# A 64x64 triangular inverse inside a decoder trunk: two products issued in four quarters of the array, the second with crossed heads

## What is computed

```python
def step(s, inp):
    r_t, w_t, k_t, v_t, z_t, bb_t = inp
    sz = jnp.einsum("bhij,bhj->bhi", s, z_t)
    s = s * w_t[:, :, None, :] + sz[..., None] * bb_t[:, :, None, :] + v_t[..., None] * k_t[:, :, None, :]
    return s, jnp.einsum("bhij,bhj->bhi", s, r_t)
```

## Time and profile before

| | |
|---|---|
| median of 3 runs | 1491.04 us |
| profiled execution, its own time | 1490.77 us |
| its span in the trace | 1489.0 us |
| TensorE (PE) busy | 1444.4 us, 97% |
| VectorE (DVE) busy | 830.7 us, 56% |
| ScalarE (ACT) busy | 509.8 us, 34% |
| chain that ended last, PE's share | 91% |

### The profile page before, as it was taken

How to read it: one execution, slowest core, us unless ns; L and a number is a source line. 1 busy time by engine, 2 the same in 40 slices (tenths; PEclk the granted TensorE clock), 3 DMA queues, 4 the chain that set the end, 5 groups by cost and what they waited for, 6 DMA issues and landing times.

```text
span 1489.0 us, 21859 instructions
## 1 busy us (share of the span) xinstructions
PE 1444.4 (97%) x9700; PEld 1191.5 (80%) x9700; DVE 830.7 (56%) x1039; ACT 509.8 (34%) x590; POOL 73.2 (5%) x67
## 2 busy tenths in 40 slices
PE   6999999998999999998999999999998999999997
PEld 5777777777888888887888888888887888888886
DVE  7768676767635354444746454455437645354455
ACT  7455454533312222223344332322424313122222
POOL 1000000013000000001200000000013000000000
PEclk9999999998999999999999999999998999999999
DMA  4111111102323222231222122123121322223221
GB/s 183 73 36 58 50 58 34 69 30 74 138 86 113 85 98 100 87 112 62 83 83 85 57 91 108 57 89 110 57 85 50 134 85 90 109 85 113 85 98 72
DMA packets 19726, 125.54 MB, mean 84 GB/s; under 512 B 2288, under 2 KB 2288, under 8 KB 5808
## 3 DMA queue, kind: packets, MB, share of 16 engines
q1 hardware_dynamic: 19088, 121.23, 22.7%
q0 software_dynamic: 544, 2.91, 0.6%
HBM read 122.03 MB, written 2.10 MB: 83 GB/s over the span
## 4 chain that ended last, share of the span: by engine, by line
PE 91%; DVE 4%; ACT 2%; issue 1%; POOL 1%; DMA 1%; SPq 0%; DVEq 0%; ACTq 0%; POOLq 0%
PE bank L339 20%; PE bank L345 20%; PE bank L342 20%; PE bank L543 4%; PE bank L540 4%; PE bank L544 4%; PE bank L1473 2%; PE bank L1476 2%; PE bank L1470 2%; PE bank L783 2%; PE bank L353 2%; PE bank L790 1%; PE bank L1506 1%; PE bank L1505 1%; PE bank L1504 1%
## 5 line engine op out<-in xcount | busy, mean ns | idle before, releaser
L339 PE MATMUL bank<-XH,WH 128*128 128x512 f32 x944 | 380.4, 403 | 24.3 <-DVE XL L432 12.6
L345 PE MATMUL bank<-XH,WL 128*128 128x512 f32 x944 | 371.6, 394 | 0.0
L342 PE MATMUL bank<-XL,WH 128*128 128x512 f32 x944 | 371.6, 394 | 0.0
L312 DVE TENSOR_TENSOR WL<-raw,WH 128x2048 fp32r<-128x2048 f32 (+1 forms) x111 | 249.7, 2251 | 174.3 <-ACT WH L306 174.2
L306 ACT ACTIVATE WH<-raw 128x2048 fp32r<-128x2048 f32 (+1 forms) x111 | 208.1, 1877 | 277.9 <-DMA raw<-weights 277.9
L339 PEld LDWEIGHTS bank<-XH,WH 128*128 128x128 f32 x944 | 180.0, 191 | 66.5 <-issue 28.3
L342 PEld LDWEIGHTS bank<-XL,WH 128*128 128x128 f32 x944 | 180.1, 191 | 38.4 <-issue 2.4
L345 PEld LDWEIGHTS bank<-XH,WL 128*128 128x128 f32 x944 | 179.6, 190 | 38.6
L656 ACT ACTIVATE AH<-relu 128x512 fp32r<-128x512 f32 x64 | 40.5, 633 | 250.0 <-DVE relu L681 250.0
L681 DVE SCALAR_TENSOR_TENSOR relu<-bank,rB 128x512 f32<-128x512 f32 x64 | 44.2, 690 | 100.0 <-PE bank L345 100.0
L339 PE MATMUL bank<-AH,WH 128*128 128x512 f32 x256 | 99.7, 389 | 0.0
(11 more groups left out here) (327 smaller groups left out, 2025.3 us busy)
## 6 DMA issues: line engine op xcount, KB each, us to landing
raw<-weights SPq DMA_DIRECT2D x107, 1024.0 KB, 4.8
raw<-weights SPq DMA_DIRECT2D x8, 512.0 KB, 4.8
h<-x_fm SPq DMA_DIRECT2D x4, 512.0 KB, 8.1
out_tm<-hT SPq DMA_DIRECT2D x8, 256.0 KB, 2.1
rc<-ret_const POOLq DMA_DIRECT2D x1, 1536.0 KB, 6.7
pp<-pairs POOLq DMA_DIRECT2D x4, 199.0 KB, 4.3
cst<-const SPq DMA_DIRECT2D x1, 577.0 KB, 12.0
gain_row<-last_gain POOLq DMA_DIRECT2D x1, 512.0 KB, 3.6
```

What stands on the lines that cost most here:

```text
L312: nc.vector.tensor_tensor(WL[i][:, :n], raw[i][:, :n], WH[i][:, :n], ALU.subtract).then_inc(S("w_lo"), 1)
L339: mm = pe.matmul(bank[b][:], wh, xh, start=(k == 0), stop=False)
L342: mm = pe.matmul(bank[b][:], wh, xl, start=False, stop=False)
L345: mm = pe.matmul(bank[b][:], wl, xh, start=False, stop=(k == len(xs) - 1))
```

## The change

Two new helpers. `kept_and_crossed` issues, for each head and chunk, a `kept` matmul and next to it one with the same stationary operand whose result goes to the partitions of the *other* head, in a second bank. `crossed_turned` is `turned` for operands that lie on the other head's partitions.

`po2` is now computed twice in one call, kept to bank 6 and crossed to bank 0. `t1z` (kept, bank 7) and `t1x` (crossed, bank 2) are one call with one signal. VectorE adds the unit to the crossed square too (new `ip2_x`, into `W[3]`), and `w2` is computed from the crossed operands. TensorE waits for `acc_free0` before the first call, for `yx_s` before `t1z`, and for `ip2_x` before `between(4)`.

```diff
+        def kept_and_crossed(pe, b, b2, lhsT, rhs, rhs2, signal):
+            for i, par, j in CH:
+                rows, cols = ROWS[j], square(par, i)
+                pe.matmul(bank[b][rows, cols], lhsT[rows, cols], rhs[rows, cols], start=True, stop=True)
+                mm = pe.matmul(bank[b2][ROWS[1 - j], cols], lhsT[rows, cols], rhs2[rows, cols], start=True, stop=True)
+            mm.then_inc(S(signal), 1)
+
+        def crossed_turned(pe, pr, lhsT, rhs, signal):
+            for i, par, j in CH:
+                rows, cols = ROWS[1 - j], square(par, i)
+                mm = pe.matmul(bank[2 * pr + j][ROWS[par], i * C:(i + 1) * C], lhsT[rows, cols], rhs[rows, cols],
+                               start=True, stop=True)
             mm.then_inc(S(signal), 1)
...
             need("po_s", "po_ts")
-            kept(pe, 6, W[0], W[1], "po2")
-            need("yz_s", "ipt")
-            kept(pe, 7, W[4], W[10], "t1z")
-            need("yx_s")
-            kept(pe, 2, W[4], W[11], "t1x")
+            pe.wait_ge(S("acc_free0"), use.now(0))
+            kept_and_crossed(pe, 6, 0, W[0], W[1], W[1], "po2")
+            need("yz_s", "yx_s", "ipt")
+            kept_and_crossed(pe, 7, 2, W[4], W[10], W[11], "t1z")
             need("k_by_token")
             by_token(pe, 1, W[6], "b_turned")
+            need("ip2_x")
             between(4)
             need("t1z_s", "ip2")
             turned(pe, 2, W[8], W[0], "w1")
-            need("t1x_s")
-            turned(pe, 3, W[8], W[1], "w2")
+            need("t1x_s", "ip2_x")
+            crossed_turned(pe, 3, W[3], W[1], "w2")
...
             nc.vector.tensor_tensor(chunked(W[8]), chunked(bank[6]), table(K_EYE2), ALU.add).then_inc(S("ip2"), 1)
-            need("t1x")
+            nc.vector.tensor_tensor(chunked(W[3]), chunked(bank[0]), table(K_EYE2), ALU.add).then_inc(S("ip2_x"), 1)
+            need("t1z")
             nc.vector.tensor_copy(W[1][:], bank[2][:]).then_inc(S("t1x_s"), 1)
```

More of the change, by code:

```diff
@@ L77 @@
     "gate_products": "gate_r gate_i",
-    "chunk_products": "azb azb_t azb_n m2 m2_t z_turned m4 e2 azk_t m8 e4 v_turned e8 x2 po po_t yz k_turned po2 t1z t1x "
+    "chunk_products": "azb azb_t azb_n m2 m2_t z_turned m4 e2 azk_t m8 e4 v_turned e8 x2 po po_t yz k_turned po2 t1z "
                       "b_turned w1 w2 gg qq",
@@ L85 @@
     "lru_factors": "lru_r lru_i lru_tanh lru_a lru_root gelu",
-    "summed_by_dve": "nn nt o nt_n m2_ts arb m4_i e2_s azk m8_i ark po_ts ipt ip2 t1x_s w2_s g_s q_s",
+    "summed_by_dve": "nn nt o nt_n m2_ts arb m4_i e2_s azk m8_i ark po_ts ipt ip2 ip2_x t1x_s w2_s g_s q_s",
     "unit_added_by_pool": "nt_i e1",
```

## The result

The changed kernel takes 1498.07 us (median of 10 runs, 1495.16 to 1505.2) against 1491.64 us for the kernel before (10 runs, 1490.84 to 1494.11): ratio 1.0039, 95% interval 1.0027 to 1.0051. It is slower, by a little more than the 0.3% that was to count as a difference, and outside the predicted range. Its profiled execution took 1495.61 us, 4.84 us more than that of before, and is the one read here.

The account below looks back on a forecast made before the run. TensorE, busy 97% of the span, was taken to bound the kernel, with instruction transfers limiting dense stretches. 1490.77 - 1.2 (TensorE's order and waits) + 1.0 (instructions, with rounding) = 1490.6 us; range 1488.3 to 1493.9.

Parts of the forecast that it names:

- The instructions, pairs 1 and 2: Instruction-block pauses in pairs 1 and 2: transfers catch up during the bank-0 wait, the 0.70 us pause only moves: 0.
- The wait itself: In pairs 1 and 2 TensorE waits for VectorE to empty bank 0 before the doubled `po2`: +0.85 us each.
- the sum over the waits behind it: Pairs 1 and 2 up to `between(4)`, counting all waits without late instruction blocks: some 0.15 us lost in each.
- Pair 0: Late instruction blocks at `w1` and in `over_tokens(0)` turn a 0.77 us gain into a loss near +0.7 us.
- Pair 3: Two old pauses go (-1.4 us), new ones come at `w1` and in `over_tokens(0)` (+0.9): -0.5 from instructions, -1.3 in all.
- The pace: The doubled `po2` and `t1z` with `t1x` run in four quarters at 14.5 ns a load, 0.93 us a call.
- The third rival: Crossed and kept matmuls on the same rows cannot overlap, so the two calls take 3.72 us: 1496.2 us, chance 0.04.
- The first rival: Instructions are never late in the chunk part: 1489.6 us, or 1487.5 with the old pauses gone; chance 0.25.
- The second rival: The one additional instruction block costs its full 3.45 us: 1493.0 us, up to 1495 with later blocks late; chance 0.17.
- the closest spacing: Instruction transfers in the chunk part follow each other at 3.45 us at the closest, 13.5 ns a record.
- stretches behind the norms: Half-clock stretches of TensorE after the residual norms differ by 3.4 us between executions, worth 1.7 us of time.

Follow-up runs that it names:

- after_shift32: Changed kernel plus 32 one-column matmuls (128 records) at TensorE's start, moving all block borders by half a block: 1498.83 us, ratio 1.0037 to the kernel before.
- wait_only: Kernel before with only the changed kernel's wait for bank 0 added ahead of the kept square: 1495.49 us, ratio 1.0022.
- hybrid: Kernel before with, in pairs 1 and 2 only, both four-quarter calls (banks 7 and 4, no bank-0 wait), `between(3)` between them: 1491.87 us, ratio 0.9982.
- after_again: The changed kernel run once more, unedited, beside the kernel before: 1500.97 us, ratio 1.0051.
- no_square: Changed kernel without crossed square or bank-0 wait, `t1z` in bank 4, `w2` using the kept square: 1494.88 us, ratio 1.0011 to the kernel before.
- ends_only: Kernel before with the four-quarter calls in pairs 0 and 3 only, crossed square in bank 7, no bank-0 wait: 1497.37 us, ratio 1.0024.

## Why the prediction was wrong

It said 1490.6 us, with a range to 1493.9, from a kernel at 1490.77; the profiled execution took 1495.61, and the median is 1498.07.

- **The instructions, pairs 1 and 2: the step that failed.** "In pairs 1 and 2 the idle time at `acc_free0` lets the transfers catch up; the pause of 0.70 moves to another border of about the same size: 0". The old pause is gone as said. But no transfer starts while TensorE stands at the wait: the next one comes behind it, and 0.40 + 0.88 us of pauses in pair 1 and 1.59 in pair 2 follow. The two pairs cost +2.98 us instead of +0.30. The earlier trace rows told how closely transfers follow each other. What starts one they did not tell, and that it starts as soon as there is time was an assumption. The traces have it 1.15 to 2.14 us behind a border at which TensorE had paused, so an idle engine, which crosses no border, lets nothing catch up.
- **The wait itself: right.** 0.85 us predicted, 0.87 measured in both pairs, ended by lines 501 and 503. after_shift32 and wait_only bear out the sum over the waits behind it: +0.18 and +0.36 with no border near, and no pause behind the wait alone, against +0.15.
- **Pair 0: right in mechanism, and nearly in size.** Late blocks at `w1` and in the loop, 0.69 and 0.90 us; +0.91 against +0.7. The size is partly luck: the 27.15 us of before is the shortest of four profiles of that form, and against the others (27.65 to 27.93) it would be +0.1 to +0.4.
- **Pair 3: a term mis-sized.** Predicted -1.3 in all; measured -0.41. The two old pauses (1.38 us) went, but the two new ones are 0.68 and 0.92, 1.60 together where 0.9 was put.
- **The pace: right.** The two calls' 128 loads go at 14.5 ns: in pair 1 the first begins at 149.53, and two windows of 0.93 and 0.94 us hold the two calls (a load that reaches into a window is counted there too, so their 61 and 73 are more than 128):

```profile
149.53:150.46 0.93, 0.90 (x57) 0.93 (x61) 0.00 (x0) 0.00 (x0) 0.00 (x0) 1.00 0.00 0
150.46:151.40 0.94, 0.94 (x80) 0.94 (x73) 0.56 (x1) 0.00 (x0) 0.00 (x0) 1.00 0.08 17
```

- **The third rival is out** with that: the crossed partner runs beside the kept one, with its rows equal. So the rule of the Trainium skill, "TensorE: Matmul & The Clock Gate", What overlaps and what doesn't, does not hold for these two products; the measurement decides.
- **The first rival is out too.** The Trainium skill, "Runtime: NRT & Kernel Launch", Instruction fetch mechanics, has fetching hidden behind the issue of instructions. Seven pauses, and their moving with a shift of the program, say otherwise for dense series of 64x64 matmuls.
- **The second rival was nearest**, and still too low by its place: the loss came behind the wait and not from the closest spacing alone. It gave 1493 to 1495 with a chance of 0.17.
- **Missing altogether: the clock.** The range had 1.7 us for stretches behind the norms, not a new one behind pair 0. At equal clock after is some 3.1 to 3.6 us over before; the medians lie 6.4 us apart. So some 3 us of the median come with the lower clock of a part of the runs. This half is an estimate with the 1.15 us per 0.001 from above, against runs of before on other chips; it is not shown, and its cause stays open.
- The uncertainty: the range ended at 1493.9, a sum of what I had found, with hardly any room for a wait and a late block in one place; my own list said that no term had room for more than 3 us, and the one term of pairs 1 and 2 took 2.7 more than was put.

## What to carry to other kernels

A new wait on an engine whose stretch is dense with small instructions costs more than its idle time where the border of a block of 256 instructions lies at the wait, a few instructions ahead of it or behind it. Here two other banks made the wait needless. Shift the program by some tiny instructions at its start before judging a gain of under 0.3%: that alone moved the chunk parts by 1.7 us. That holds for the hybrid too: four-quarter calls with a large matmul between them in pairs 1 and 2 alone are the most promising form here, but its 0.18% was measured at one place of the borders.

## What the runs showed of the hardware

- TensorE's program comes in blocks of 256 instructions (88 pauses, all at multiples of 256 from each other). In the profiles of before and after a block was usable 2.2 to 2.8 us after its transfer started, where TensorE had paused for it. Behind each pause of after the next transfer started 1.15 to 2.14 us after TensorE had crossed the border, and a semaphore wait 18 instructions behind a border put it off to 3.5 us (pair 2: border at 223.73, wait over at 226.26, transfer at 227.2, pause of 1.59 us to 229.82).
- A stretch of 10.2 to 13.6 us at 1.2 GHz can stand behind the dense part of pair 0 (after_again 85.9 to 99.5, no_square 88.0 to 98.2, ends_only 86.0 to 96.2), though in after_again TensorE was idle for only 2.7 of the 10.9 us before it. It is there in some executions of a program and not in others, and the three profiles that have it are the only ones at a mean clock of 0.983.
- Two matmuls of 64x64 on the same rows and into different column halves ran at 14.5 ns a weight load when four quarters were in use, as fast as pairs on different rows.
